# Hybrid conformer / PEER step: gathered rows for one token tile in both expert products, VectorE splits weights while gates are built

## Chip, cores and metric

One Trainium2 chip (trn2), one core. The metric is the device time of one execution in microseconds (us); the number given for a kernel is the median of its runs.

## What is computed (the reference, cut)

One layer, 512 + 32 = 544 tokens, width 2048, all float32. RMSNorm, one input projection, a conv branch and a differential-attention branch, a gated merge, an output projection with residual. Then the PEER channel mixer:

```
q  = h2 @ w_pq                          # 8 heads, two halves of 64
s1, s2 = q1 . sub_k1, q2 . sub_k2       # 128 keys each
v1, i1 = top16(s1); v2, i2 = top16(s2)
sc, j  = top16(v1[a] + v2[b])           # of 256 candidates
idx    = i1 * 128 + i2                  # 16384 experts
a      = einsum('td,thkd->thk', h2, u_tab[idx])
wgt    = softmax(sc) * gelu(a)
out    = einsum('thk,thkd->td', wgt, v_tab[idx])
```

Each token picks 8 x 16 = 128 experts of 16384.

## The kernel before

The 544 tokens lie on the free axis. Weights stream from `w_all` in 368 units of 1 MB (128 x 2048 float32), through two slots: SyncE loads a slot (`load_w`, L316), ScalarE rounds it to float32r (`hi`, L546), GpSimd or VectorE subtracts to get the low half (`lo` L482, `split` L1196), and TensorE multiplies high x high, low x high and high x low (`product`, L1271 to L1284). In the slot of unit m, unit m + 2 is prepared once m is done. The stages, in order:

1. **z stage**, 72 units, nine for each of the eight heads. VectorE empties PSUM (`evac`, L784), does rotary, softmax pieces and the 31 taps of the conv; between units' matmuls TensorE runs hooks (statistics, scores, transposes, values) that wait for VectorE and ScalarE. Beside each weight load SyncE copies two 1 MB units of `peer_v` inside DRAM (`rows_of`, L331) into a table with one expert per row, `v_rows`.
2. **Merge and out**, 16 + 16 units; each out unit gives `x2` and, at once, `h2_hi`/`h2_lo` without the norm's factor `rs2`, which is applied later: on `qp` (L1029) and, by GpSimd, on every result of the U stage (L500).
3. **peer_wq**, 8 units, then the **U stage**: 128 units, each the dot products of 128 experts with all 544 tokens, as two 272-column matmuls per weight tile (`u_unit`, L1485). ScalarE copies the result out of PSUM (L708), GpSimd scales it, ScalarE applies Gelu and stores it to `a_scr`. During the first 40 units VectorE does top-k for five token tiles, one per 8 units (L1064 to L1128); TensorE takes each tile's choices (`choices_t`, L1506) inside the seventh unit of the tile. Then 13 rounds of 6 units: VectorE makes one-hot rows for 32 tokens per round (L1147 to L1149) and TensorE multiplies them into gate tables (L1532); VectorE adds the two halves of the result into `g_st` (L1162, L1164).
4. **V stage**, 128 units in 16 groups of 8, for 416 tokens by 416-column matmuls (`v_group`, L1545), where VectorE prepares gate x activation (`prep`), adds each tile (L1192) and splits the weights. The first tile of 128 tokens (tokens 416 to 543) is done otherwise: GpSimd fetches each token's chosen rows of `v_rows` by indirect DMA (L506) and the chosen activations one by one from `a_scr` (L513), VectorE multiplies these by the gates (`weigh`, L1202) and accumulates the rows in PSUM (`gather_add`, L1208), nine rows a group.

Engines run in program order, so whatever stands behind a waiting instruction waits too.

## Time and profile before

| what | value |
|---|---|
| median of 3 runs | 4459.39 us (4457.0 to 4462.22) |
| the profiled execution | 4454.38 us, span 4452.6 us |
| mean granted TensorE clock | 0.989 |
| PE / DVE / ACT / POOL busy | 98% / 67% / 24% / 39% |
| DMA over the span | 822.58 MB, mean 185 GB/s |

The span runs from the first to the last instruction; 1.8 us lie outside it. Busy shares are means over stages with different limits, so the stretches and the timelines are read beside them.

### The profile page before, as it was taken

To read this page: it belongs to the slowest core of one execution; us is meant where nothing else is said; L and a number is where in the kernel's file an instruction comes from. 1 tells how busy PE (TensorE), PEld (TensorE's weight loads), DVE (VectorE), ACT (ScalarE), POOL (GpSimd) and SP (SyncE) were. 2 spreads that over 40 slices of the span, in tenths; PEclk is the share of its full clock that TensorE was granted. 3 is DMA by queue.
4 is the path that set the end of the run, shared out by engine and by line. 5 is a ranking of instruction groups with operands and counts; after the bars stand their busy time and mean duration, and the time that the engine had idled before them with its cause. 6 is when DMAs were issued, how large, how long until landed. Compare 5 with 4: busy or idle time off the path is not lost.

```text
span 4452.6 us, 78681 instructions
## 1 busy us (share of the span) xinstructions
PE 4351.6 (98%) x30758; PEld 4276.9 (96%) x30758; DVE 3003.3 (67%) x4653; ACT 1079.1 (24%) x1100; POOL 1758.2 (39%) x639
## 2 busy tenths in 40 slices
PE   8999999999999999999999999999989999999999
PEld 7999999999999999999999999999989999999999
DVE  5767656676762256557888888886268777877774
ACT  3332323322211122222222222222212121221221
POOL 3323323332333344444444444444544433444420
PEclk9999999999999999999999999999999999999999
DMA  6656566564333322222333333333577767776763
GB/s 241 235 191 229 197 234 229 188 227 164 106 136 135 110 95 108 108 106 102 133 126 136 131 130 135 134 135 128 198 277 264 291 261 292 266 296 258 282 253 126
DMA packets 332184, 822.58 MB, mean 185 GB/s; under 512 B 23152, under 2 KB 230768, under 8 KB 264688
## 3 DMA queue, kind: packets, MB, share of 16 engines
q1 hardware_dynamic: 279968, 608.53, 39.0%
q0 software_dynamic: 22528, 134.30, 7.4%
q10 hardware_dynamic: 29520, 77.40, 4.5%
q8 instruction: 119, 1.95, 0.2%
q14 instruction: 49, 0.40, 0.0%
HBM read 734.72 MB, written 219.66 MB: 214 GB/s over the span
## 4 chain that ended last, share of the span: by engine, by line
issue 56%; PE 21%; POOL 18%; DMA 3%; DVE 1%; POOLq 0%; ACT 0%; DVEq 0%; SPq 0%; ACTq 0%
PE pair L1557 21%; POOL w_lo L482 13%; POOL ab L500 4%; DMA a_el<-a_scr,a_idx 3%; POOL vg L506 1%; DVE ST L1208 1%; DVE acc L1192 0%; POOL a_el L513 0%; DMA xs<-x_t 0%; POOL xsq L488 0%; POOLq L481 0%; ACT h_hi L552 0%; POOLq L497 0%; POOLq L492 0%; DVE w_lo L1196 0%
## 5 line engine op out<-in xcount | busy, mean ns | idle before, releaser
L482 POOL TENSOR_TENSOR w_lo<-w_raw,w_hi 128x2048 fp32r<-128x2048 f32 x242 | 1118.0, 4620 | 1114.6 <-ACT w_hi L546 1114.6
L1280 PE MATMUL pair<-h_hi,w_hi 128*128 128x272 f32 x6656 | 1397.5, 291 | 12.8 <-issue 12.8
L1280 PE MATMUL pair<-h_hi,w_lo 128*128 128x272 f32 x6656 | 1381.5, 289 | 0.0
L1280 PE MATMUL pair<-h_lo,w_hi 128*128 128x272 f32 x6656 | 1377.0, 288 | 0.0
L1280 PEld LDWEIGHTS pair<-h_hi,w_hi 128*128 128x128 f32 x6656 | 1048.2, 189 | 21.1 <-issue 13.9
L1280 PEld LDWEIGHTS pair<-h_lo,w_hi 128*128 128x128 f32 x6656 | 1048.5, 189 | 0.0
L546 ACT ACTIVATE w_hi<-w_raw 128x2048 fp32r<-128x2048 f32 x368 | 703.8, 1913 | 1417.3 <-PE pair L1557 858.4
L1280 PEld LDWEIGHTS pair<-h_hi,w_lo 128*128 128x128 f32 x6656 | 1044.7, 189 | 0.0
L1557 PE MATMUL pair<-wt_hi,w_hi 128*128 128x416 f32 x2048 | 727.3, 355 | 49.4 <-DVE acc L1192 48.3
L1557 PE MATMUL pair<-wt_hi,w_lo 128*128 128x416 f32 x2048 | 728.7, 356 | 0.0
L1557 PE MATMUL pair<-wt_lo,w_hi 128*128 128x416 f32 x2048 | 722.6, 353 | 0.0
L506 POOL DMA_INDIRECT vg<-v_rows,v_idx x128 | 321.1, 2508 | 595.7 <-DVE ST L1208 584.9
L500 POOL TENSOR_TENSOR ab<-ab,rs 128x544 f32<-128x544 f32 x128 | 178.7, 1396 | 791.0 <-ACT ab L708 791.0
L1557 PEld LDWEIGHTS pair<-wt_hi,w_hi 128*128 128x128 f32 x2048 | 389.7, 190 | 57.3 <-DVE acc L1192 53.2
L1557 PEld LDWEIGHTS pair<-wt_lo,w_hi 128*128 128x128 f32 x2048 | 390.3, 191 | 6.3
L1557 PEld LDWEIGHTS pair<-wt_hi,w_lo 128*128 128x128 f32 x2048 | 389.5, 190 | 3.2
L708 ACT ACTIVATE ab<-pair 128x544 f32<-128x544 f32 x128 | 80.1, 626 | 1203.5 <-PE pair L1280 1203.5
L1148 DVE TENSOR_SCALAR oh<-late_sb,i_t,g_hi 128x128 fp32r<-128x128 f32 x416 | 356.5, 857 | 0.0
L877 DVE SCALAR_TENSOR_TENSOR xg<-u,params_sb,xg 128x512 f32<-128x512 f32 x464 | 338.6, 771 | 23.3 <-DVE xg L875 1.3
L1192 DVE TENSOR_TENSOR acc<-pair,acc 128x416 f32<-128x416 f32 x256 | 149.4, 588 | 277.0 <-PE pair L1557 218.0
L1208 DVE SCALAR_TENSOR_TENSOR ST<-vg,w_g,ST 128x2048 f32<-128x2048 f32 x128 | 300.6, 2348 | 2.9 <-DVE w_g L1202 2.9
L1196 DVE TENSOR_TENSOR w_lo<-w_raw,w_hi 128x2048 fp32r<-128x2048 f32 x126 | 287.9, 2285 | 13.3 <-ACT w_hi L546 13.3
(223 smaller groups left out, 3999.6 us busy)
## 6 DMA issues: line engine op xcount, KB each, us to landing
w_raw<-w_all SPq DMA_DIRECT2D x368, 1024.0 KB
v_rows<-w_all SPq DMA_DIRECT2D x128, 1024.0 KB, 8.8
a_scr<-gb ACTq DMA_DIRECT2D x128, 272.0 KB, 2.1
g_scr<-g_st ACTq DMA_DIRECT2D x26, 1024.0 KB, 4.1
a_st<-a_scr SPq DMA_DIRECT2D x16, 1664.0 KB, 8.4
gl_st<-g_scr SPq DMA_DIRECT2D x16, 1664.0 KB
gate_scr<-zb ACTq DMA_DIRECT2D x32, 272.0 KB, 2.2
gt<-gate_scr SPq DMA_DIRECT2D x32, 272.0 KB, 3.4
```

Source lines behind the costliest of these rows:

```text
L482: pool.tensor_tensor(w_lo[:, slot, :], raw[:, slot, :], w_hi[:, slot, :].bitcast(F32), ALU.subtract)\
L500: pool.tensor_tensor(ab[:, n, :], ab[:, n, :], rs2[:, :], ALU.mult).then_inc(ab_scaled, 1)
L506: pool.indirect_dma_start(vg[j % NVG][:, :], None, v_rows.rearrange("g c p d -> (g c p) d"), bass.IndirectOffsetOnAxis(v_idx[:, j:j + 1], ...
L546: act.activation(w_hi[:, slot, :], raw[:, slot, :], ACT.Copy).then_inc(hi_ready, 1)
L708: act.activation(two(ab[:, n, :]), PV[n], ACT.Copy).then_inc(ab_full, 1)
L877: own.by(V.scalar_tensor_tensor(xg[:, a:b], src, cw, xg[:, a:b], ALU.mult, ALU.add))
L1148: V.tensor_scalar(oh1[:, sl, 0, :], iota, c1, g_hi[:, bass.ds(t, 1)].bitcast(F32), ALU.is_equal, ALU.mult)
L1192: V.tensor_tensor(acc[:, d, 0:NT], PD[k], acc[:, d, 0:NT], ALU.add).then_inc(acc_added, 1)
L1196: V.tensor_tensor(w_lo[:, slot, :], raw[:, slot, :], w_hi[:, slot, :].bitcast(F32), ALU.subtract)\
L1208: V.scalar_tensor_tensor(acc_g, vg[x % NVG][:, :], w_g[:, bass.ds(s0 + x, 1)], acc_g, ALU.mult, ALU.add)\
L1280: last = mm(out[:, f, :], a, b[:, k, f * HT:(f + 1) * HT], start=(x == 0 and y == 0), stop=(x == n - 1 and y == 2))
L1557: last = mm(PD[k], a, r_[b][:, c, :], start=(c == 0 and y == 0), stop=(c == GRP - 1 and y == 2))
```

## The change

- **U stage for 416 tokens only.** `u_unit` now issues one 416-column matmul where there were two of 272. ScalarE applies Gelu straight from PSUM; the copy, GpSimd's scaling and `ab` are gone.
- **The other 128 tokens from fetched rows.** Each of their 128 dot products a token is made by VectorE (`dot`) from a row that GpSimd fetches, against `h2_g`, the tokens' `h2` turned to rows in PSUM by TensorE (`h2_turned`, 16 x 4 x 2 plain float32 matmuls with 32 columns). Nine dots stand in each of the 13 gate rounds, eleven behind them. The single-element fetches and `weigh` are gone; one Gelu and one multiply make `w_g`.
- **A row table for `peer_u`.** In the z stage SyncE loads each of the 128 units of `peer_u` into SBUF (`u_load`), VectorE transposes it in 32 x 32 blocks (`turn`, two ahead of each of the first sixteen `evac` of every eighteen), and SyncE stores it (`u_store`, four DMAs). For the room, the conv output and `o_lo` go to DRAM in the z stage and are loaded at the start of the merge, where the conv mean's matmuls now stand in the first unit's second tile.
- **The `v_rows` copies move** out of the z stage: 32 into the merge, 32 into the out units, two per unit over the eight peer_wq units and the first eight U units, one per unit over the 32 U units after.
- **h2 with its norm.** VectorE writes `h2_s`; when `rs2` is there it scales each of the 16 tiles, ScalarE rounds it, VectorE makes the low half, and the first two peer_wq units run side by side over k, waiting for each tile.
- **Low halves.** GpSimd makes them until the gate rounds (units up to 42 of U) and for the last 7 of U and first 2 of V; VectorE makes the 78 in the rounds (`split`) and, as before, those of the V stage.
- **Gates.** One plain float32 matmul of 128 columns a token where there was a float32r one of 256; ScalarE (`gate_copy`) empties PSUM instead of VectorE's copy and add. The rounds begin after 42 units.

```diff
-NVG = 3
+NG = 3
+DOTS = 9
...
+        UA = [PA[:, 2 * n, 0:NT] for n in range(2)]
+        PD = [ST[:, k, 0:NT] for k in range(2)]
         SV, TOV = S[:, :, 0:HT], TO[:, :, 0:HT]
...
+            def u_store(hp, i):
+                for q in range(4):
+                    sp.dma_start(u_rows[bass.ds(hp * 32 + i, 1), :, :, q, :].rearrange("a b i n -> i (a b) n"),
+                                 u_out[32 * q:32 * q + 32, i % 2, :].rearrange("p (b n) -> p b n", b=4)).then_inc(u_stored[i % 2], 16)
...
+                        for k in range(2):
+                            if n <= 16:
+                                sp.wait_ge(u_turned, hp * 32 + (2 * n + k + 1))
+                            if n < 16:
+                                u_load(hp, 2 * n + k)
+                            if 1 <= n <= 16:
+                                u_store(hp, 2 * n + k - 2)
...
+            g_end = (NQ + U_G0 + BU * NGB) // 2 + 2
+            pq_pu_loads(0, GRP, lambda v, n: [rows_at(v, NGRP // 4, GRP // 2 + 2 * n + k) for k in range(2)])
+            for g in range(NGRP // 4):
+                b0 = GRP + 4 * g
+                pq_pu_loads(b0, b0 + 4, lambda v, n: rows_late(v - b0, 3 * NGRP // 4 + g, n))
...
+                if j >= NG:
+                    pool.wait_ge(row_taken, j - NG + 1)
+                table = u_rows.rearrange("c b i q n -> (c b i) (q n)") if j < SLOTS else v_rows.rearrange("g c p d -> (g c p) d")
+                pool.indirect_dma_start(rows[j % NG][:, :], None, table,
+                                        bass.IndirectOffsetOnAxis(v_idx[:, j % SLOTS:j % SLOTS + 1], 0))\
+                    .then_inc(row_loaded[j % NG], 16)
...
+            for s in u_stored:
+                pool.wait_ge(s, 64 * NKEY // 2 + 1)
+            pool.wait_ge(scores_taken, TT)
+            pool.wait_ge(chosen, TT)
+            j = 0
+            for v in range(NGB // 2):
+                for k in range(3):
+                    for i in range(DOTS // 3):
+                        fetch(j)
+                        j += 1
+            w = U_PU + U_G0 + BU * NGB + 1
+            while w < U_PV + 2:
+                pool.wait_ge(lo_ready, w)
...
+                    if j < SLOTS:
...
-                act.activation(two(ab[:, n, :]), PV[n], ACT.Copy).then_inc(ab_full, 1)
+                act.wait_ge(a_stored[n], v * 16 + 1)
+                act.activation(gb[:, n, :], src[n], ACT.Gelu).then_inc(ab_full, 1)
                 hi(v + (U_PU // 2 + 1), n)
...
+                V.transpose(u_out[:, i % 2, :].rearrange("p (b k j) -> p k b j", b=4, k=KD), u_in[:, i % 2, :])\
+                    .then_inc(u_turned, 1)
...
+                for k in range(2):
+                    if ZPH * r + i < 16:
+                        turn(hp, 2 * (ZPH * r + i) + k)
...
+            for k in range(KD + 1):
+                if k < KD:
+                    V.tensor_tensor(h2_s[:, k, :], h2_s[:, k, :], rs2[:, :], ALU.mult).then_inc(h2_scaled, 1)
+                if k > 0:
+                    dve.wait_ge(h2_rounded, k)
+                    V.tensor_tensor(h2_lo[:, k - 1, :], h2_s[:, k - 1, :], h2_hi[:, k - 1, :].bitcast(F32), ALU.subtract)\
+                        .then_inc(h2_ready, 1)
...
-                    V.tensor_scalar(oh1[:, sl, 0, :], iota, c1, g_hi[:, bass.ds(t, 1)].bitcast(F32), ALU.is_equal, ALU.mult)
-                    ins = V.tensor_scalar(oh1[:, sl, 1, :], iota, c1, e_t[:, bass.ds(t, 1)], ALU.is_equal, ALU.mult)
+                    ins = V.tensor_scalar(oh1[:, sl, :], iota, c1, e_t[:, bass.ds(t, 1)], ALU.is_equal, ALU.mult)
...
+            def split(un, slot):
+                dve.wait_ge(hi_ready, un + 1)
+                dve.wait_ge(lo_ready, un)
+                V.tensor_tensor(w_lo[:, slot, :], raw[:, slot, :], w_hi[:, slot, :].bitcast(F32), ALU.subtract)\
+                    .then_inc(lo_ready, 1)
...
+                j = v * DOTS + i
+                dve.wait_ge(row_loaded[i % NG], v * (16 * DOTS // NG) + 16 * (i // NG + 1))
+                buf = rows[i % NG]
+                V.scalar_tensor_tensor(buf[:, :], buf[:, :], 1.0, h2_g, ALU.mult, ALU.mult,
+                                       accum_out=dot_g[:, bass.ds(j, 1)]).then_inc(row_taken, 1)
...
+                un = v * 6 + (U_PU + U_G0 + 1)
+                dots = iter(range(DOTS))
+                for b in range(2):
+                    for i in range(BU):
+                        split(un + (BU * b + i), (BU * b + i + 1) % 2)
+                        dot(v, next(dots))
+                        next_hot(4 * b + i)
+                        if i < 2 - b:
+                            dot(v, next(dots))
+                    next_hot(4 * b + 3)
...
+            dve.wait_ge(h2g_ready, 1)
...
+            for i in range(SLOTS - NGB // 2 * DOTS):
+                dot(NGB // 2, i)
...
+            dve.wait_ge(a_g_ready, 1)
+            own.by(V.tensor_tensor(w_g[:, :], gate_g[:, :], a_el[:, :], ALU.mult))
...
+            pe.wait_ge(osum_ready, 1)
+            spread(S, ones, osq).then_inc(ostat_ready, 1)
...
+            for k in range(KD):
+                pe.wait_ge(h2_ready, k + 1)
+                for n in range(2):
+                    wh, wl = (w[:, n, k * P:(k + 1) * P] for w in (w_hi, w_lo))
...
+                    if k == KD - 1:
+                        last.then_inc(unit_done, 1)
...
+                for k in range(KD):
+                    wh, wl = (w[:, n, k * P:(k + 1) * P] for w in (w_hi, w_lo))
+                    for y, (a, b) in enumerate(((wh, h2_hi), (wh, h2_lo), (wl, h2_hi))):
+                        last = mm(dst[n], a, b[:, k, 0:NT], start=(k == 0 and y == 0), stop=(k == KD - 1 and y == 2))
...
+                for k in range(KD):
+                    for q in range(4):
+                        for y, src in enumerate((h2_hi, h2_lo)):
+                            last = mm(PA[:, q, 32 * k:32 * k + 32], src[:, k, NT:T].bitcast(F32), ident[:, 32 * q:32 * q + 32],
+                                      start=(y == 0), stop=(y == 1))
+                last.then_inc(h2g_ready, 1)
...
+                            out = ST[:, 2 + gq % 2, :].rearrange("p (c t) -> p c t", t=4)[:, :, t]
+                            last = mm(out, oh2[:, sl, :], oh1[:, sl, :], start=True, stop=True)
```

## Rows read from the trace of the kernel before

**Rows 1.** Stretches (us, busy us of each engine, clock, DMA share, GB/s).

```profile
35.00:1100.00 1065.00, 1047.72 (x7816) 998.93 (x7816) 701.19 (x996) 318.54 (x474) 330.68 (x72) 0.99 0.61 210
...
1604.00:3217.00 1613.00, 1611.56 (x12878) 1609.51 (x12878) 1161.93 (x2526) 404.14 (x413) 768.71 (x256) 1.00 0.35 127
3217.00:4452.00 1235.00, 1183.95 (x6160) 1166.46 (x6160) 892.40 (x887) 243.64 (x128) 456.02 (x258) 0.98 0.70 261
```

**Rows 2.** Timeline of ScalarE, two unit ends in the tail of the U stage.

```profile
3179.95 0.63 ACT L708 ACTIVATE ab<-pair 128x544 f32<-128x544 f32 x1 [9.05 <-PE pair L1280]
...
3191.97 0.63 ACT L708 ACTIVATE ab<-pair 128x544 f32<-128x544 f32 x1 [9.05 <-PE pair L1280]
```

**Rows 3.** Timeline of ScalarE, unit ends while the gate matmuls run.

```profile
2511.79 0.63 ACT L708 ACTIVATE ab<-pair 128x544 f32<-128x544 f32 x1 [9.69 <-PE pair L1280]
...
2549.87 0.62 ACT L708 ACTIVATE ab<-pair 128x544 f32<-128x544 f32 x1 [9.69 <-PE pair L1280]
```

**Rows 4.** Timeline of PE, V stage, 55 matmul starts apart.

```profile
3863.76 0.35 PE L1557 MATMUL pair<-wt_lo,w_hi 128*128 128x416 f32 x1
...
3874.17 0.35 PE L1557 MATMUL pair<-wt_hi,w_lo 128*128 128x416 f32 x1
```

**Rows 5.** The page's part 5, TensorE in the V stage and VectorE's long operations.

```profile
L1557 PE MATMUL pair<-wt_hi,w_hi 128*128 128x416 f32 x2048 | 727.3, 355 | 49.4 <-DVE acc L1192 48.3
...
L1208 DVE SCALAR_TENSOR_TENSOR ST<-vg,w_g,ST 128x2048 f32<-128x2048 f32 x128 | 300.6, 2348 | 2.9 <-DVE w_g L1202 2.9
L1196 DVE TENSOR_TENSOR w_lo<-w_raw,w_hi 128x2048 fp32r<-128x2048 f32 x126 | 287.9, 2285 | 13.3 <-ACT w_hi L546 13.3
```

**Rows 6.** Waits in the V stage, summed (us, times, longest).

```profile
DVE w_g L1202 <- DMA a_el<-a_scr,a_idx: 89.7, 14, 14.3
```

**Rows 7.** Timeline of PE, plain f32 matmuls of the attention (two instructions each).

```profile
1033.86 0.61 PE L1378 MATMUL ST<-a_t,v_tok 128*128 128x128 f32 x4
1034.39 0.91 PE L1347 MATMUL ST<-kn_t,q_t 64*128 64x384 f32 x2
...
685.40 0.53 PE L1381 MATMUL ST<-a_t,pv 128*128 128x32 f32 x4
685.86 0.40 PE L1382 MATMUL ST<-a_t,v_smp 32*128 32x32 f32 x2
```

**Rows 8.** Timeline of VectorE, one top-k tile, first copy to last reduction.

```profile
1707.89 1.22 DVE L1066 COPY sc<-ST 128x1024 f32<-128x1024 f32 x1 [20.32 <-PE ST L1499]
...
1759.15 6.22 DVE L1112 TENSOR_TENSOR wk<-jf,late_sb 128x2048 f32<-128x2048 f32 x1
...
1767.73 2.29 DVE L1120 TENSOR_REDUCE isel<-wk 128x128 f32<-128x2048 f32 x1
```

**Rows 9.** Timeline of GpSimd, the low half of one unit's weights.

```profile
1722.53 4.63 POOL L482 TENSOR_TENSOR w_lo<-w_raw,w_hi 128x2048 fp32r<-128x2048 f32 x1 [0.43 <-ACT w_hi L546]
```

**Rows 10.** Timeline of VectorE, end of a head; then ScalarE, its unit's end.

```profile
704.25 0.72 DVE L808 TENSOR_TENSOR zb<-pair,rs 128x544 f32<-128x544 f32 x1
...
696.52 1.92 ACT L546 ACTIVATE w_hi<-w_raw 128x2048 fp32r<-128x2048 f32 x1 [2.38 <-PE pair L1280]
```

**Rows 11.** The page's parts 3 and 6, DMA queues and the row copies.

```profile
q1 hardware_dynamic: 279968, 608.53, 39.0%
...
v_rows<-w_all SPq DMA_DIRECT2D x128, 1024.0 KB, 8.8
```

**Rows 12.** Timeline of VectorE and GpSimd between the out units and peer_wq.

```profile
1503.68 0.72 DVE L1009 SCALAR_TENSOR_TENSOR x<-pair,xt 128x544 f32<-128x544 f32 x1 [8.23 <-PE pair L1280]
...
1514.08 3.55 DVE L1024 RECIPROCAL rs<-rs 128x544 f32<-128x544 f32 x1 [2.02 <-ACT rs L695]
...
1507.08 4.67 POOL L482 TENSOR_TENSOR w_lo<-w_raw,w_hi 128x2048 fp32r<-128x2048 f32 x1 [7.18 <-ACT w_hi L546]
```

**Rows 13.** Groups of VectorE by line, the one-hot rows (busy us, mean ns).

```profile
L1149 DVE TENSOR_SCALAR oh<-late_sb,i_t,e_t 128x128 fp32r<-128x128 f32 x416 | 184.4, 443 | 0.0
...
L1147 DVE TENSOR_SCALAR oh<-late_sb,i_t 128x128 fp32r<-128x128 f32 x416 | 155.8, 375 | 0.0
```

More of the change, by code:

```diff
@@ L158, in build @@
         rs1 = az.take("rs1", [P, T])
+        c_ts = az.take("c_ts", [P, TS])
         xs = Area(Y0, HALF).take("xs", [P, KD, T])
@@ L225, in build @@
         g_st = aw.take("g_st", [P, 2, NKEY, GB])
-        oh2 = aw.take("oh2", [P, 8, NKEY], F32R)
-        oh1 = aw.take("oh1", [P, 8, 2, NKEY], F32R)
+        oh2 = aw.take("oh2", [P, 16, NKEY])
+        oh1 = aw.take("oh1", [P, 16, NKEY])
         avx, avy = Area(X0, BIG), Area(Y0, BIG)
         acc = avx.take("acc", [P, KD, T])
+        rows = [avy.take(f"rows{i}", [P, DM]) for i in range(2)] + [rows2]
         a_st = avy.take("a_st", [P, GRP, NT])
@@ L397, in _ @@
                 merge_loads(v, KD, 0)
+                for n in range(GRP // 2):
+                    rows_at(v, 0, n)
             with sp.Fori(0, NC_ // 2) as v:
                 merge_loads(v, 0, KD)
+                for n in range(GRP // 2, GRP):
+                    rows_at(v, 0, n)
             sp.wait_ge(m_taken, 2 + 2 * KD)
@@ L404, in _ @@
                 for n in range(2):
+                    for k in range(GRP // 4):
+                        rows_at(v, NGRP // 4, n * (GRP // 4) + k)
                     sp.wait_ge(lo_ready, v * 2 + (n + 1 + U_OUT))
@@ L518, in _ @@
[L518 to L532 removed]
+            lo(U_PU + U_G0, 0)
@@ new lines, in _ @@
+            for s in u_stored:
+                pool.wait_ge(s, 64 * NKEY // 2 + 1)
[10 more added lines that the diff above has]
+                pool.wait_ge(lo_ready, w)
+                lo(w, w % 2)
+                w += 1
+                for i in range(2):
+                    if j < SLOTS:
+                        fetch(j)
+                        j += 1
@@ L535, in _ @@
+            pool.wait_ge(rows_stored, 16 * NV)
+            for j in range(SLOTS, 2 * SLOTS):
+                fetch(j)
         @block.scalar
@@ L1218, in group @@
             def group(g, parity, more, slots, splits, pre=None):
-                s0, full, rounds, n_slots = slots
+                s0, rounds, n_slots = slots
                 for n in range(GRP):
@@ L1233, in group @@
                             prep(1 - parity, 2 * (n - 3) + 1)
-                    if n == 0 and n_slots:
-                        weigh(parity, s0 + parity * PER_GRP, full, n_slots)
-                        settle()
                     if n < n_slots:
@@ L1411, in _, with mean @@
                         product(PV[n % 2], n % 2, 0, range(KD), h_hi, h_lo, order(hooks, i)).then_inc(unit_done, 1)
-            pe.wait_ge(std_ready, 3 * NH + 2)
-            pe.wait_ge(conv_done, NH + 1)
-            for k in range(KC):
-                last = spread(S, ones, c_all[:, k, :], start=(k == 0), stop=(k == KC - 1))
-            last.then_inc(mean_ready, 1)
             pe.wait_ge(zb_full, NZ + 2)
             pe.wait_ge(norm_done, 3 * NH + 1)
+            pe.wait_ge(o_loaded[0], 16)
+            def mean():
+                pe.wait_ge(std_ready, 3 * NH + 2)
+                pe.wait_ge(c_loaded, 16)
+                for k in range(KC):
+                    last = spread(S, ones, c_all[:, k, :], start=(k == 0), stop=(k == KC - 1))
+                last.then_inc(mean_ready, 1)
             def merge_unit(v, n, unit0, rhs_hi, rhs_lo, hooks=None):
@@ L1426, in merge_unit @@
                     product(PV[k], n, KC * k, range(KC), rhs_hi, rhs_lo, hooks and hooks[k]).then_inc(tile_done, 1)
-            with pe.Fori(0, NA // 4) as v:
+            for n in range(2):
+                merge_unit(0, n, 0, o_hi, o_lo, ({KC - 2: lambda: pe.wait_ge(o_loaded[1], 16)}, {KC - 1: mean}) if n == 0 else None)
+            with pe.Fori(1, NA // 4) as v:
                 for n in range(2):
@@ L1474, in _ @@
                 pe.wait_ge(x2_ready, n + 1 + NO)
-                hooks = {7: rms2, KD - 2: lambda: pe.wait_ge(h2_ready, KD)} if n == 0 else None
-                product(PV[n], n, 0, range(KD), h2_hi, h2_lo, hooks).then_inc(unit_done, 1)
+            for k in range(KD):
+                pe.wait_ge(h2_ready, k + 1)
+                for n in range(2):
+                    wh, wl = (w[:, n, k * P:(k + 1) * P] for w in (w_hi, w_lo))
+                    for y, (a, b) in enumerate(((wh, h2_hi), (wh, h2_lo), (wl, h2_hi))):
+                        for f in range(2):
+                            last = mm(PV[n][:, f, :], a, b[:, k, f * HT:(f + 1) * HT],
+                                      start=(k == 0 and y == 0), stop=(k == KD - 1 and y == 2))
+                    if k == KD - 1:
+                        last.then_inc(unit_done, 1)
             with pe.Fori(1, NQ // 2) as v:
@@ L1565, in _ @@
             for d in range(KD):
-                last = nc.tensor.transpose(ST[:, d // 4, (d % 4) * GT:(d % 4 + 1) * GT], vg[0][:, d * P:(d + 1) * P], ident)
+                last = nc.tensor.transpose(PA[:, d // 4, (d % 4) * GT:(d % 4 + 1) * GT], rows[0][:, d * P:(d + 1) * P], ident)
             last.then_inc(acc_g_turned, 1)
```

282 lines of the change are left out of this document (139 added, 143 removed).

## Prediction, made before the changed kernel was run

> **What bounds the kernel now.** I read first the busy time by stretch, then TensorE's pace inside each stage, then who waits for whom. In the U stage TensorE is busy 1611.56 of 1613 us at a clock of 1.00 [rows 1]: nothing but its own instructions sets the time there. In the V stage it is busy 1183.95 of 1235 us [rows 1], and the missing 50 us are waits for VectorE's adds, 48.3 us [rows 5], which stand behind `weigh`, waiting 14 times and 89.7 us for single fetched elements [rows 6]. The z stage is nearly full too (1047.72 of 1065 us), but VectorE is at 701.19 us and the DMA engines at 0.61 there [rows 1]. So a gain has to come out of TensorE's columns in U, and whatever is loaded onto VectorE and the DMAs in z has to fit there.
>
> **The paces.** A U unit takes 3191.97 - 3179.95 = 12.02 us [rows 2] for 96 matmuls of 272 columns, 0.125 us each. A 416-column matmul takes 10.41 / 55 = 0.1893 us [rows 4]; 48 of them make a unit of 9.09 us. While gates run, a unit takes (2549.87 - 2511.79) / 3 = 12.69 us [rows 3], 0.67 us more, so all 78 units pay 52 us for gates.
>
> **U stage, term by term.**
> - The products: 128 x (12.02 - 9.09) = **-375**.
> - Gates: 416 matmuls of plain float32, two instructions each. Four instructions of 128 columns took 1034.39 - 1033.86 = 0.53 us [rows 7], so 0.265 a token, 110 us for 52: **+58**. The lower bound is the four 32-column instructions, 0.46 us [rows 7], which would give 96 us (+44).
> - `h2_turned`: 16 x 4 x 2 matmuls of two instructions, 256 x 0.115 = 29 us [rows 7], bare, because the round's first split and dot wait for it: **+29** (34 at the 128-column pace).
> - Top-k: from first copy to last reduction a tile takes 1767.73 + 2.29 - 1707.89 = 62.1 us on VectorE [rows 8]. TensorE takes the choices a quarter into the seventh unit, now after 6.25 x 9.09 = 56.8 us instead of 75. Part of the 62.1 is blocking: the second L1112 took 6.22 us [rows 8] where the like-sized L1196 takes 2.285 [rows 5], and it ends when a GpSimd low half ends. GpSimd still does one such 4.63 us operation a unit [rows 9], so I keep 61. Four tiles stall by 4: **+17** (0 to 30). The first tile has no such hook.
> - Low halves: with GpSimd the slot of a unit is ready 0.5 + 1.9 + 4.6 = 7.0 us (Gelu, a little less than the 0.63 of 544 columns [rows 2]; rounding [rows 10]; low half [rows 9]) after the unit before ends, against 9.09. Hidden, with 2 us to spare; VectorE's two-input operations can hold GpSimd off by 2.3, so some tenths a tile. In the last eight units GpSimd has a low half and two fetches to do, near 9 us: **+2**.
> - DMA at the start: two copies, a weight load and a store are 3.36 MB a unit of 9.5 us (scores included), 354 GB/s, where q1 moved 608.53 MB in 39.0% of 4452.6 us, 350 GB/s [rows 11]: **+5** (0 to 10).
> Sum for U: **-264**.
>
> **The gate rounds on VectorE.** A round of TensorE is 6 x 9.09 + 32 x 0.265 = 63.0 us. VectorE has six splits of 2.285, nine dots of about 2.35 [rows 5] and 32 pairs of one-hots, at most 0.375 + 0.443 = 0.82 us a pair [rows 13], blocked ones included: 13.7 + 21.1 + 26.2 = 61 us, and about 50 when GpSimd no longer blocks. Each split is due 5 us before TensorE needs it. So I cost this at nothing; the cover is 2 to 13 us a round. Rows cannot run dry: nine a round is one per 7 us with three buffers, and V already fetches one per 9 us. ScalarE's `gate_copy`, Gelu and rounding are near 3 us of a 10.5 us unit.
>
> **V stage.** `weigh` goes: the 48.3 us of stalls, and with them the clock that falls behind them (0.98 over the stage against 1.00 in U [rows 1], so short times at the lower of its two levels, 1.2 instead of 2.4 GHz): TensorE was busy 1183.95 us where 6144 x 0.1893 is 1163, 21 us too long. What is late next is the first row of V, fetched only after GpSimd's last low half (7 us into V) and needed before VectorE's split for the third unit: about 5 us. **-62** (-50 to -69).
>
> **Out to peer_wq.** h2 can't be used before `rs2`. The last x2 begins at 1503.68 and the reciprocal ends at 1514.08 + 3.55 [rows 12], of which about 4.4 us are a copy blocked by the GpSimd operation of 1507.08 [rows 12]; with one VectorE operation fewer ahead of it that copy just slips past. Scale, round and subtract add 2.2. TensorE idles about 11.5 us, and 16 if the copy is caught. Then both first units end together and GpSimd must finish the next slot, 6.7 us more. Clock recovery about 4. **+22** (16 to 32).
>
> **z to merge.** The last head's conv output and `o_lo` go out and come back (2.5 MB behind one another) before the seventh k tile of the first product: **+8** (0 to 15). The mean's matmuls only move. The `v_rows` copies in merge and out I cost at nothing: two a unit of 12 us or more is what z carried beside its loads at a share of 0.61 [rows 1].
>
> **z stage, the uncertain term.** No row shows a `turn`. From below it is 2.285 us, the f32 operation over as many elements [rows 5]; from above twice that, 4.6. I take 2.3: one input, no conversion. The Trainium skill has the only price of it: Vector Engine (DVE) Microarchitecture Reference, section 3.8, says that the transposing front end is "Pipelined to sustain one element per cycle per lane"; an estimate by it is the time of any other operation over 2048 elements at that rate, and the sum would stay. VectorE has 701.19 / 8 = 87.6 us a head of 133 [rows 1]; sixteen turns make it 124. They stand before `evac`, partly in time that VectorE waits. But at a head's end VectorE is late already: `evac` of the ninth unit began at 704.25, while the unit had ended by 696.52 [rows 10]; there the turns push it to some 13 us late, past a unit's 12.02, and in between softmax weights miss their hooks by 0.5 to 2 us each. Following one head through I get some 6 us of TensorE waits: 48. DMA: z moved 1065 x 210 = 224 MB; less 134 of copies, plus 268 in and out and 4, is 362 MB. At 210 / 0.61 = 344 GB/s [rows 1] that is 1052 us busy, 92% of the longer stage, and a turn waits for its load and for its buffer's store: 16. The clock falls at some of the new stalls: 16. **+80** (+15 to +200).
>
> **Sum.** -264 - 62 + 22 + 8 + 80 = -216. The profiled execution took 4454.38 us (span 4452.6); the median of the runs is 4459.39, 5.0 more. 4454.4 - 216 = 4238, as a median **4243 us**.
>
> **Rivals.**
> - *z absorbs the turns* (12%): VectorE's waits in z, 365 us by the busy time [rows 1], swallow 295 us of turns; +15 instead of +80: 4178. Against it: the late `evac` [rows 10].
> - *z becomes bound by VectorE and the DMA chain together* (12%): load, turn and store have two buffers each and both resources are above 90%; +190: 4353.
> - *The rounds become bound by VectorE* (7%): a round of 70 us instead of 63, because dots wait for rows or splits come behind one-hots: 13 x 7 = 91: 4334.
> - *The end on the other side: the turn is dear* (7%). Without z the change is at -296, 37 us a head. VectorE's head is 87.6 + 16 turns + some 8 us of waits that nothing can fill; it reaches 133 + 37 at a turn of 4.6 us. From there the kernel is slower; at 5.5 us z grows by 8 x (183.6 - 133) = 405: 4568. Only a transpose at less than half the rate of any like operation here [rows 5] does that.
> - *Memory bandwidth* (4%). A copy inside DRAM reads and writes: a unit of peer_wq and the first eight of U would move 5.45 MB at the memory. If that ran at the 336 GB/s that z shows in this count ((224 + 134) / 1065) it would be 16 us a unit instead of 12 and 9.5, 85 us in all: 4328. The copies landed 8.8 us after issue [rows 11], and a load and two copies go out within some 1.5 us: over 500 GB/s, so I give it little. The Trainium skill speaks for it: SBUF — State Buffer, "A bandwidth-pool intuition that's wrong", puts HBM to one core at ~358 GB/s; by that the estimate is 15.2 us a unit and +71. The 8.8 us row disagrees.
>
> **Chances.** Forecast 58%, its own range 4195 to 4300. The range to hold 8 of 10 takes in the first three rivals: **4165 to 4375**. About 0.2%, 9 us, is what can be told from no change. Faster 0.92, same 0.01, slower 0.07, the dear turn being the only case that ends there.
>
> **What would show it.** Right: U units 9.09 us apart; rounds of 63 us; turns of 2.3 us; V groups 72.7 us apart with no wait for acc; TensorE idle some 12 and 7 us around the first peer_wq units; z longer by 40 to 120 us with waits of TensorE for VectorE's values in the later units of a head. Wrong: turns above 3 us; DMA share of z at 0.97 or more; rounds above 66 us with VectorE busy; weight loads late (ScalarE waiting for w_raw) in z or at the start of U.

## The result, and the profile after

The changed kernel took **4356.7 us** (median of 4 runs, 4353.33 to 4363.76), the kernel before 4458.19 beside it (median of 4 runs): a ratio of 0.9775 (0.9758 to 0.9792), 101.5 us faster. The prediction was 4243 us, 216 faster, with a range of 4165 to 4375: the direction was right and the time lies in the range, but the gain is 101.5 us where 216 were forecast.

Where it went is read from the times at which TensorE begins each stage (merge: its first product; U: the first scores; V: its first product):

| stage | before | after | difference | forecast |
|---|---|---|---|---|
| z, to merge's first product | 1100.5 | 1249.6 | +149 | +80, and part of the +8 |
| merge, out, peer_wq | 503.9 | 540.0 | +36 | +22, and the rest of the +8 |
| U | 1612.7 | 1380.2 | -232 | -264 |
| V, to the end | 1235.5 | 1181.3 | -54 | -62 |

TensorE began merge behind a wait of 2.30 us before and of 9.26 us after:

```profile
1100.51 0.64 PE L1280 MATMUL pair<-o_hi,w_hi 128*128 128x272 f32 x2 [2.30 <-DVE zb L808]
```

```profile
1249.63 0.82 PE L1376 MATMUL PA<-o_hi,w_hi 128*128 128x272 f32 x2 [9.26 <-DVE zb L903]
```

The stretches of the profile after, which answer to [rows 1] (start and end in us, length, busy time and instruction count of each engine, granted clock, DMA share, GB/s):

```profile
35.00:1241.00 1206.00, 1073.74 (x7784) 1014.33 (x7784) 927.85 (x1120) 314.20 (x473) 325.94 (x71) 0.95 0.87 304
1249.00:1789.00 540.00, 506.23 (x3880) 501.85 (x3880) 224.15 (x247) 105.59 (x80) 180.76 (x39) 0.96 0.81 280
1789.00:3169.00 1380.00, 1341.72 (x7406) 1323.29 (x7406) 989.99 (x2229) 377.63 (x388) 370.53 (x182) 0.97 0.75 271
3169.00:4351.00 1182.00, 1167.10 (x6160) 1155.28 (x6160) 890.25 (x874) 241.76 (x126) 304.32 (x125) 0.99 0.73 276
```

The z stage was nearly full before, 17 us idle in 1065. Now TensorE idles 132 of 1206 us there, and its work takes 26 us longer at a clock of 0.95. U was full before; now 38 us of it are idle. Who makes it wait, over the whole span (who waits <- for whom: total us, times, longest):

```profile
PE ST L1390 <- ACT sq L646: 52.9, 12, 12.7
PE ST L1461 <- DVE e L946: 46.7, 17, 5.4
PE PA L1376 <- DVE zb L903: 16.9, 5, 9.3
PE ST L1631 <- DVE isel L1215: 14.4, 4, 3.6
PE ST L1682 <- DVE wt_lo L1291: 12.6, 1, 12.6
PE PA L1376 <- issue: 11.9, 3, 4.4
PE ST L1390 <- ACT xsq L615: 11.9, 1, 11.9
PE ST L1598 <- POOL w_lo L542: 11.6, 1, 11.6
PE ST L1682 <- DVE acc L1295: 11.0, 1, 11.0
```

The first two are z. ScalarE's square is late because VectorE's evac is; in each of the four passes (two heads each) TensorE stood 11 to 13 us at the second head's first statistics. Of the third, 9.3 us are the seam of z and merge. The fourth is top-k. The sixth stands between the passes of z, the seventh at the kernel's start, and the rest at seams between stages. The costliest groups of VectorE on the page that are new:

```profile
L872 DVE STREAM_TRANSPOSE u_out<-u_in 128x2048 f32<-128x2048 f32 x128 | 291.1, 2296 | 105.9 <-DMA u_rows<-u_out 92.3
L1253 DVE SCALAR_TENSOR_TENSOR rows<-rows,PA 128x2048 f32<-128x2048 f32 x128 | 291.9, 2281 | 53.8 <-DMA rows<-u_rows,v_idx 53.8
```

A turn takes 2.296 us, as assumed, so the dear turn (the case on the slow side) is out. The Trainium skill (Vector Engine (DVE) Microarchitecture Reference, section 3.8) has a transpose at one element per cycle and lane, and the trace agrees: `dot`, over as many elements, takes 2.281. But the turns also *waited* 92.3 us for stores of the table, which is VectorE's time as well.

`h2_turned` is the next surprise. The view of instructions of 2200 to 2290 us, and the stretch of 2220 to 2240:

```profile
L1608 PE MATMUL PA<-consts_sb,h_lo 128*128 128x32 f32 x128 | 36.9, 380 | 0.0
L1608 PE MATMUL PA<-consts_sb,h_hi 128*128 128x32 f32 x128 | 36.7, 379 | 0.0
```

```profile
2220.00:2240.00 20.00, 20.00 (x96) 20.00 (x95) 0.00 (x0) 0.00 (x0) 0.00 (x0) 0.50 0.12 50
```

The 256 instructions ran from 2211.7 to 2261.7 us, 50 us and not 29: 96 of them in 20 us at a granted clock of 0.50, the lower level of 1.2 GHz, with TensorE never idle. In the 10 us before the block the clock was 1.00.

The gate rounds went as forecast: ScalarE's Gelus of seven units in a row lie (2760.4 - 2698.4) / 6 = 10.33 us apart, 62.0 us a round against 63.0.

```profile
L779 ACT ACTIVATE gb<-ST x7: 517/517/521, 2698.4 to 2760.4; 128x416 f32<-128x416 f32 x7
```

At the seam of U and V the timeline of TensorE shows three stalls that end within 57 us (start, length, instruction, idle time before it and what ended it):

```profile
3136.42 0.71 PE L1598 MATMUL ST<-h_hi,w_hi 128*128 128x416 f32 x1 [11.56 <-POOL w_lo L542]
...
3169.80 0.71 PE L1682 MATMUL ST<-wt_hi,w_hi 128*128 128x416 f32 x1 [12.59 <-DVE wt_lo L1291]
...
3192.85 0.72 PE L1682 MATMUL ST<-wt_hi,w_hi 128*128 128x416 f32 x1 [11.00 <-DVE acc L1295]
```

All three go back to loads that came late. The weight unit behind the loads for V's first group landed late, so its low half was late. GpSimd's next row fetch stands behind that low half, VectorE's dot waited for the row, and the first preparation stands behind the dots. VectorE's first add of V waited for `acc`, which SyncE loads behind the second group's loads:

```profile
3129.73 1.91 ACT L606 ACTIVATE w_hi<-w_raw 128x2048 fp32r<-128x2048 f32 x1 [13.29 <-DMA w_raw<-w_all]
```

```profile
3143.70 2.29 DVE L1253 SCALAR_TENSOR_TENSOR rows<-rows,PA 128x2048 f32<-128x2048 f32 x1 [15.86 <-DMA rows<-u_rows,v_idx]
...
3192.20 1.09 DVE L1295 TENSOR_TENSOR acc<-ST,acc 128x416 f32<-128x416 f32 x2 [22.44 <-DMA acc<-x_scr]
```

### The profile page after: what moved, and what is told of

It is laid out like the page before. It is cut to its first block, busy times and chain, and to the rows that moved or that the text cites. A ratio compares the mean times of both kernels' runs of the same rounds, so it can differ in the third digit from the quotient of the medians.

```text
span 4351.1 us, 69418 instructions
## 1 busy us (share of the span) xinstructions
PE 4106.5 (94%) x25286; PEld 4007.7 (92%) x25286; DVE 3063.5 (70%) x4486; ACT 1059.2 (24%) x1090; POOL 1207.5 (28%) x433
## 4 chain that ended last, share of the span: by engine, by line
PE 53%; issue 33%; POOL 6%; DVE 6%; DMA 1%; SPq 0%; ACT 0%; POOLq 0%; DVEq 0%; ACTq 0%
PE ST L1682 27%; PE ST L1598 18%; POOL w_lo L542 6%; PE PA L1598 3%; PE ST L1657 2%; PE PA L1376 2%; PE PA L1608 1%; DVE wk L1207 1%; DMA w_raw<-w_all 1%; DVE cand L1177 1%; DVE wk L1211 0%; DVE isel L1215 0%; DVE ti L1173 0%; DVE ti L1176 0%; DVE wk L1169 0%
## 5 line engine op out<-in xcount | busy, mean ns | idle before, releaser
L1682 PE MATMUL ST<-wt_hi,w_hi 128*128 128x416 f32 x2048 | 719.5, 351 | 23.6 <-DVE wt_lo L1291 12.6
L1682 PE MATMUL ST<-wt_hi,w_lo 128*128 128x416 f32 x2048 | 724.5, 354 | 0.0
L1682 PE MATMUL ST<-wt_lo,w_hi 128*128 128x416 f32 x2048 | 716.5, 350 | 0.0
L1376 PE MATMUL PA<-h_hi,w_hi 128*128 128x272 f32 x2496 | 546.4, 301 | 25.6 <-issue 11.9
L1598 PE MATMUL ST<-h_hi,w_hi 128*128 128x416 f32 x1408 | 533.4, 379 | 11.6 <-POOL w_lo L542 11.6
L1376 PE MATMUL PA<-h_hi,w_lo 128*128 128x272 f32 x2496 | 524.4, 292 | 0.0
L1376 PE MATMUL PA<-h_lo,w_hi 128*128 128x272 f32 x2496 | 524.3, 292 | 0.0
L1598 PE MATMUL ST<-h_lo,w_hi 128*128 128x416 f32 x1408 | 499.4, 355 | 0.0
L1598 PE MATMUL ST<-h_hi,w_lo 128*128 128x416 f32 x1408 | 496.7, 353 | 0.0
L1376 PEld LDWEIGHTS PA<-h_hi,w_hi 128*128 128x128 f32 x2496 | 404.7, 194 | 34.9 <-issue 27.1
L872 DVE STREAM_TRANSPOSE u_out<-u_in 128x2048 f32<-128x2048 f32 x128 | 291.1, 2296 | 105.9 <-DMA u_rows<-u_out 92.3
```

The costliest lines, as they stand in the source:

```text
L872: V.transpose(u_out[:, i % 2, :].rearrange("p (b k j) -> p k b j", b=4, k=KD), u_in[:, i % 2, :])\
L1376: last = mm(out[:, f, :], a, b[:, k, f * HT:(f + 1) * HT], start=(x == 0 and y == 0), stop=(x == n - 1 and y == 2))
L1598: last = mm(dst[n], a, b[:, k, 0:NT], start=(k == 0 and y == 0), stop=(k == KD - 1 and y == 2))
L1682: last = mm(PD[k], a, r_[b][:, c, :], start=(c == 0 and y == 0), stop=(c == GRP - 1 and y == 2))
```

## Experiments: what the table costs in the z stage

Theory V says that VectorE's time and order make z longer, theory D that the DMAs do. The first three runs take the new work of the z stage apart: without both turns and moves (loads and stores), with the turns alone, and with the moves alone.

**No table.**

```diff
-                        for k in range(2):
-                            if n <= 16:
-                                sp.wait_ge(u_turned, ...)
...
-                for k in range(2):
-                    if ZPH * r + i < 16:
-                        turn(hp, 2 * (ZPH * r + i) + k)
-                table = u_rows... if j < SLOTS else v_rows...
+                table = v_rows...
```

> The z stage of the changed kernel without the table of peer_u: no loads, no turns, no stores. The dot products of the first tile fetch from v_rows in place of u_rows, so they are left wrong, at the same cost. In the changed kernel the first product of the merge starts at 1249.6 us of the span, in the kernel before at 1100.5. Both theories (VectorE's order, DMA traffic) say that the whole difference of 149 us is the table's: merge from 1100 to 1110 us, and the time 4210 to 4225 us. If the conv output and o_lo that go out to DRAM cost in the z stage, the merge starts later than 1120.

**Turns only.** As above, but the turns stay and read two units that are loaded once.

> The z stage with all 128 turns on VectorE, but no loads and stores of the table (two units are loaded once, and each turn reads them again; the dot products fetch from v_rows and are wrong). Theory V, VectorE's time and order: the turns stand ahead of evac, 128 x 2.3 us on VectorE, and the heads' last units are late by them; merge starts at 1200 to 1240 us, the time is 4305 to 4345. Theory D, the DMAs: turns waited 92.3 us for stores of u_rows and the queues are at a share of 0.87; merge starts at 1110 to 1150 us, the time is 4215 to 4255.

**Moves only.**

```diff
-                V.transpose(u_out[:, i % 2, :].rearrange("p (b k j) -> p k b j", b=4, k=KD), u_in[:, i % 2, :])
+                V.transpose(u_out[:, i % 2, 0:32], u_in[:, i % 2, 0:32])
```

> The z stage with all loads and stores of the table, but each turn cut to 32 of its 2048 columns, so that VectorE has all waits and almost none of the work (the table is left wrong). Theory V: merge starts at 1105 to 1140 us, time 4210 to 4245. Theory D: merge starts at 1190 to 1240 us, time 4295 to 4345. A result in the middle of both this run and the one without moves says that both are needed, each adding to the other.

They took 4187.45, 4253.91 and 4295.32 us (2 runs each). The first product of merge, in the same order:

```profile
1085.43 0.82 PE L1362 MATMUL PA<-o_hi,w_hi 128*128 128x272 f32 x2 [9.25 <-DVE zb L889]
```

```profile
1148.51 0.82 PE L1370 MATMUL PA<-o_hi,w_hi 128*128 128x272 f32 x2 [9.26 <-DVE zb L895]
```

```profile
1175.63 0.82 PE L1379 MATMUL PA<-o_hi,w_hi 128*128 128x272 f32 x2 [8.33 <-DVE zb L903]
```

The table costs 1249.6 - 1085.4 = 164 us of z. That is 15 more than the difference to the kernel before, for without the table z is 15 us shorter than before (1085.4 against 1100.5). The turns alone cost 63 and the moves alone 90, together 153 of the 164: neither theory has it alone, and my expectations for the two single runs were both too one-sided. The run without table came out below its range too (4187 against 4210 to 4225). The changed kernel's own merge began between 1249.6 and 1261.0 us in five profiles, so the 11 us between 153 and 164 say nothing. The moves cost far more than the 16 us that I gave to the DMAs. How they do it stands in VectorE's group for the turns of the third run, 35 to 1100 us:

```profile
L872 DVE STREAM_TRANSPOSE u_out<-u_in 128x32 f32<-128x32 f32 x122 | 23.4, 203 | 191.2 <-DMA u_rows<-u_out 179.3 <-issue 10.7 <-DMA u_in<-w_all 0.8
```

The turns, of 0.2 us each, still wait 179.3 us in all for the store of two turns ago, and they stand *ahead of evac*. So a late transfer is passed on to VectorE, evac and TensorE.

**Other places for the turns.** None at the ninth unit of a head, two in each of the first eight, and in the first two units behind evac.

```diff
-                for k in range(2):
-                    if ZPH * r + i < 16:
-                        turn(hp, 2 * (ZPH * r + i) + k)
+                if 2 <= i < 8:
+                    turns()
...
                     V.tensor_tensor(two(zb[:, j, :]), PV[j], two(rs1[:, :]), ALU.mult).then_inc(zb_full, 1)
+                if i < 2:
+                    turns()
```

> The changed kernel with other places for the turns, nothing else: none at the ninth unit of either head, two in each of the first eight; those of a head's first two units stand behind evac, in VectorE's wait for ScalarE's rstd, in place of ahead of it. The stall of 11 to 13 us in each of the four passes, at the second head's first statistics, stands behind evac of the ninth unit and four turns. Theory V: it goes, and some of the others shrink, 35 to 60 us less, 4295 to 4320. Theory D: the same bytes in the same time, within 10 us of 4357.

4285.79 us, ratio to before 0.9610 (0.9594 to 0.9626): 71 us less than the changed kernel, with the same work and the same bytes. Merge began at 1181.3, and the 11 to 13 us stalls were gone. TensorE's waits and VectorE's, 35 to 1165 us:

```profile
PE ST L1466 <- DVE e L951: 43.8, 15, 5.6
PE ST L1428 <- DVE zb L906: 11.1, 8, 2.3
```

```profile
DVE u_out L872 <- DMA u_rows<-u_out: 77.2, 42, 3.9
```

**Moves only, in these places.** Both edits together.

> The turns moved in pairs, each cut to 32 columns: all loads and stores, VectorE free of the work (the table is left wrong). With full turns in these places merge started at 1181.3 us; with cut turns in the old places at 1175.6; without the table at 1085.4. If the bytes (DMA share 0.9) bound the z stage: merge at 1165 to 1180 here too, 4268 to 4284. If the waits for loads and stores only count with VectorE's own work and place: merge at 1100 to 1130, 4205 to 4235.

4250.16 us (2 runs), and merge began at 1124.0:

```profile
1124.02 0.82 PE L1384 MATMUL PA<-o_hi,w_hi 128*128 128x272 f32 x2 [9.25 <-DVE zb L906]
```

All the bytes of the table fit in a z stage only 39 us longer than without them, at a DMA share of 0.93 (35 to 1115 us), so the bytes alone don't make the 1181.3 of the run with full turns. The whole account of z, in us over the run without table:

| places of the turns | turns only | moves only | both |
|---|---|---|---|
| as changed | 63 | 90 | 164 |
| moved | not run | 39 | 96 |

The places cost 68 of the 164 us, shown by one edit. Which part of it does this (none at the ninth unit, or the first two behind evac) no run splits. What is left, 96, is about the moves' 39 and the turns' 63, but that 63 was measured in the old places.

**Turns one by one.** The 16 turns of a head spread through the head, and each store issued ahead of the next load; then the same with the old order of load and store.

```diff
+                    evac(hp, r, 0)
+                    TN(0)
+                    rope(h, 0)
+                    TN(1)
...
+                        att_max(g + s, s)
+                        TN(2 * s + 4)
+                        att_mix(g + s, s)
+                        TN(2 * s + 5)
```

> The changed kernel with its 16 turns a head spread one by one through the head: behind evac and rope, in VectorE's wait for the exponentials between the maximum and the mix of the first two tiles, and behind each mix of the last three; SyncE issues each store ahead of the next load. With the turns moved in pairs merge started at 1181.3 us, 96 later than without the table, and with cut turns at 1175.6. If what is left there is the bytes (DMA share 0.91 to 0.92), this run gains nothing on that one: 4280 to 4290 us. If it is turns that stand in pairs and wait for a store just issued (73.8 us of waits there), merge starts at 1140 to 1165 and the time is 4250 to 4275.

> The run with the turns spread one by one, but with SyncE's old order, each load ahead of the store. That run was 13 us slower than the changed kernel, its turns waiting 173 us for loads, where stores went first. If the order of load and store did that: at or below the run with turns moved in pairs, 4270 to 4290. If the single places did it: 4350 or more.

The first missed both of its cases: 4369.75 us (ratio 0.9803, 0.9788 to 0.9818). The second, 4346.63 (0.9764, 0.9745 to 0.9782), came 3 us under the one for single places, 4350 or more. With stores first VectorE waited for loads instead; with loads first, again for stores (35 to 1240 and to 1165 us):

```profile
DVE u_out L872 <- DMA u_in<-w_all: 173.0, 47, 15.0
```

```profile
DVE u_out L872 <- DMA u_rows<-u_out: 92.6, 39, 4.1
```

The order of load and store is worth 23 us, by these two runs. With the same order, the single places lose 61 us against the pairs moved. Some of that is at the stage's end, where TensorE stood 30.0 us ahead of merge in place of 9.3. That the last head's turns, now behind its last evac, hold back the loads of `o_lo` and the conv output is my reading; no run isolates it.

## Experiments: h2_turned and the seam

**h2_turned in 16 pieces**, one behind each k step of the unit (`{k: (lambda k=k: h2_turned(k)) for k in range(KD)}` in place of `{KD - 1: h2_turned}`).

> The changed kernel with h2_turned cut into 16 pieces of 16 matmuls, one behind each k step of the unit that it stood behind. The same 256 matmuls took 50 us there in one block at a granted clock of 0.56, and 0.115 us each is 29 us. Theory C, the clock: among matmuls of 416 columns it stays at 1.00 and the unit takes 9.1 + 29 us: 20 to 25 us less than the changed kernel, 4332 to 4337. Theory I, the pitch of 0.195 us is each matmul's own, with its weight load: no change within 8 us of 4357.

4370.41 us (0.9808, 0.9792 to 0.9823), neither theory's number, and the U stage 5 us *longer* (1385.5). The clock fell here too, and the wide matmuls between the narrow ones slowed with it. A stretch in the middle of the unit:

```profile
2240.00:2250.00 10.00, 10.00 (x44) 9.87 (x43) 0.00 (x0) 0.00 (x0) 0.00 (x0) 0.50 0.00 0
```

**h2_turned by 128 columns.**

```diff
                 for k in range(KD):
-                    for q in range(4):
-                        for y, src in enumerate((h2_hi, h2_lo)):
-                            last = mm(PA[:, q, 32 * k:32 * k + 32], src[...], ident[:, 32 * q:32 * q + 32], ...)
+                    for y, src in enumerate((h2_hi, h2_lo)):
+                        last = mm(PA[:, k // 4, P * (k % 4):P * (k % 4 + 1)], src[...], ident, ...)
...
+            for q in range(4):
+                own.by(V.tensor_copy(stage[:, q], turned[:, q]))
+            settle()
+            V.tensor_copy(h2_g, rows2[:, :]).then_inc(h2g_placed, 1)
```

> The changed kernel with h2_turned as 32 plain float32 products of 128 columns in place of 128 of 32; VectorE then puts the result in the order of the rows with four copies through the third row buffer and one back, about 5 us, beside TensorE's next unit. Cut in pieces, the 256 narrow matmuls brought the granted clock down to 0.50 inside a unit of 416-column matmuls, so the narrow ones themselves are the suspect. Theory N, the number of narrow instructions sets the cost: 64 instructions of 128 columns at 0.13 us are 8.5 us where 50 were, 35 to 42 us less, 4315 to 4322 us. Theory F, plain float32 of any width brings the clock down: the block takes 17 us and the next unit is slow too, 20 to 28 us less.

4333.19 us (0.9731, 0.9716 to 0.9746), 23.5 less. The stage itself gained more: U took 1332.7 us against 1380.2, 47.5 less, but z and what follows it took 12 us more in this run than in the changed kernel's profile with the same code, and V 12 more. The same values moved by 64 instructions, in stretch 2220 to 2230, with the clock at 1.00:

```profile
2220.00:2230.00 10.00, 10.00 (x81) 9.98 (x80) 0.47 (x1) 2.31 (x2) 2.37 (x3) 1.00 0.85 322
```

By the whole time alone this would be theory F's number (20 to 28 us); the stage and the clock decide for N, whose 35 to 42 us were short by 5. The block is short, though, 7 us. The gate rounds of the changed kernel have 32 such products a round, each alone among nine wide matmuls, and the clock stays at 1.00 there; a long unbroken block of 128-column plain float32 is in no run:

```profile
2290.00:3079.00 789.00, 789.00 (x4480) 780.25 (x4479) 603.29 (x1085) 233.98 (x253) 111.71 (x113) 1.00 0.82 303
```

**The seam of U and V.**

```diff
-            load_ag(0)
-            pq_pu_loads(g_end, (NQ + NU) // 2)
+            for v in range(g_end, (NQ + NU) // 2):
+                for n in range(2):
+                    sp.wait_ge(lo_ready, v * 2 + (n + 1 + U_PQ))
+                    load_w(v + (U_PQ // 2 + 1), n)
+                    if v == g_end:
+                        (load_a, load_gl)[n](0)
...
             for c in range(GRP):
                 prep(0, c)
+                if c % 2:
+                    dot(NGB // 2, tail - 4 + c // 2)
```

> The changed kernel with another order at the seam of U and V: the first group's a and gates are loaded one behind each of two weight units, not both ahead of them; VectorE prepares the first group between the last four dot products and clears acc_g behind that; behind the seam the first weight units and x2 go ahead of the second group's a and gates. In the changed kernel TensorE waited 11.56 us for a low half at 3136, 12.59 for the first preparation and 11.00 for acc. If the order of the queue and of VectorE makes them: 20 to 30 us less, 4327 to 4337. If it is the bytes at that place, whatever the order: within 10 us of 4357.

4344.6 us (0.9743, 0.9727 to 0.9760): 12 less, half of what I expected. The stall for acc was gone and the one for the first preparation was 9.34 us, but one of 11.73 us for a low half stood in U as before. A new wait had taken the old one's place: the first preparation waited for `gl_st`, the four dots stood behind it, and GpSimd's next fetch, which stands ahead of a low half in its program, waited for a row buffer:

```profile
3146.19 0.59 DVE L1301 TENSOR_TENSOR a_st<-a_st,gl_st 128x416 f32<-128x416 f32 x1 [17.79 <-DMA gl_st<-g_scr]
```

```profile
3151.84 1.06 POOL L580 DMA_INDIRECT rows<-u_rows,v_idx  x1 [16.95 <-DVE rows L1267]
```

**All three.** Turns one by one with stores first, h2_turned in pieces, and this seam.

> The three edits together (turns spread, h2_turned in pieces, seam of U and V reordered). They lie in three stages, so their gains should add: 4357 less what each gives alone, about 4357 - 90 - 22 - 25 = 4220 us, within 10 us of the sum of the single gains.

4363.21 us (0.9790, 0.9777 to 0.9804). Single differences of +13, +14 and -12 add to 4372; the edits add within 9 us, but two of them were losses.

**The best version.** Turns moved in pairs, h2_turned by 128 columns, the seam with all dots ahead of the first preparation and `gl_st` loaded first, and `{9: choices_t}` for `{3: choices_t}` (with `{5: gate_sums}` for `{1: gate_sums}`).

> Turns moved in pairs, h2_turned by 128 columns, the seam of U and V reordered with all dots ahead of the first preparation, and the token tiles' choices taken at the tenth instead of the fourth k step. Gains over the changed kernel in its own stages: 71 us, some 38, some 20 and 4 x 3.6 = 14: 4357 - 143 = 4214 us, 4200 to 4230 if they add.

**4214.38 us** (5 runs, 4209.54 to 4219.78), 0.9458 (0.9445 to 0.9471): as expected, 142 us below the changed kernel, with nothing of the computation left out. The sum fits better than its terms: between the two profiles z lost 70 us, U 77 and V nothing (1184.6 against 1181.3), where 71, 52 and some 20 for the seam had been added up. U takes 1303.4 us, 29 less than with the 128-column turn alone; merge starts at 1179.9. Of the U stage's 11.6 us for a low half 3.7 are left, of 14.4 for choices 0.8, and the first waits for acc come to 12.6 us in eight pieces, the longest 2.6.

**The changed kernel again, and two more turns moved.** In the last run two turns of each head stand in VectorE's waits for the first two tiles' exponentials.

> The changed kernel, unaltered, on the same chip as the run beside it: the time of merge's start there is the spread of the z stage between chips. 4353 to 4368 us; merge starts at 1247 to 1262 us.

> The run with all four edits, and in z two turns of each head moved out of the pairs ahead of the fourth and fifth evac into VectorE's waits for the first two tiles' exponentials (3.7 and 2.3 us there). In that run TensorE waited 45.5 us, 16 times, for attention weights, above all 5.2 to 5.7 us for the third tile's in each head. If VectorE's order makes that wait: it shrinks to some 1 to 3 us, 16 to 35 us less, 4180 to 4200 us, merge at 1145 to 1165. If bytes bound the stage by now: the wait moves elsewhere, within 8 us of 4214.

4360.76 us (0.9781, 0.9764 to 0.9797), with merge at 1256.5, and 4209.86 (4199.93 to 4217.69; 0.9447, 0.9428 to 0.9465), which the spread can't tell from the best version. The turns' waits for stores went from 74.5 to 137.7 us, and TensorE's for attention weights only from 45.5 to 38.2 (35 to 1150 us of both):

```profile
DVE u_out L888 <- DMA u_rows<-u_out: 137.7, 54, 5.3
```

```profile
PE ST L1492 <- DVE e L969: 38.2, 16, 4.2
```

A turn that comes earlier only waits longer for its output buffer's store, so VectorE's order no longer makes the wait: the 4180 to 4200 us of that case didn't come, the "within 8 us of 4214" of the other did. I read it as the chain of store and turn through two buffers that holds z there. The share of the DMA engines is 0.91 in both runs, so the bytes remain a rival. A third output buffer would tell them apart; it wasn't tried.

## Why the prediction was right or wrong

- **z, +80: the step that failed.** The term was built of 48 us of late VectorE, 16 of DMA waits and 16 of clock. The turns alone cost 63 us, near 48 and some clock. But the moves alone cost 90, where I had 16. I had "a turn waits for its load and for its buffer's store" in the text, and priced it as a small extra on a busy resource. The runs showed in its place that each wait is inserted into VectorE's program ahead of evac and delays all that is behind; of the cost, 68 us are the places alone, and with the new places the 11 to 13 us stalls behind a head's end are gone, where [rows 10] had shown VectorE already late. The clock took more than 16: from the run without table to the changed kernel TensorE's busy time in z goes from 1033.87 to 1073.74 us for the same number of matmuls, 40 us, at 1.00 and 0.95. The run without table, to lay beside the first stretch above:

```profile
35.00:1076.00 1041.00, 1033.87 (x7786) 986.31 (x7784) 697.59 (x992) 315.14 (x472) 326.90 (x72) 1.00 0.27 94
```

- The rival "z bound by VectorE and the DMA chain together" gave 4353, and the time was 4356.7. That the numbers meet is luck: it had +190 for z where +149 came, and the other stages fell 46 us short of their sum. Its mechanism, two buffers and both resources loaded, is the nearest of all. Its claim that both are above 90% isn't: the DMA share is 0.87, and VectorE is busy for 77% of the stretch. The waits in VectorE's program did it, and no share shows a full resource.
- **U, -264: -232.** The difference of 32 is a net one: three terms below were 43 us too small (21 for `h2_turned`, 10 for the late low half, 12.6 ahead of V), others some 21 too large (the rounds 13 times 1 us, the DMAs 5, top-k 3); the 10 us left I can't place. The products came as forecast (Gelus of units without extra work 8.98 and 9.15 us apart, 9.07 in the mean, against 9.09), the rounds with 62.0 for 63.0, top-k with 3.6 us for 4 a tile. The +5 for the DMAs at the start doesn't show: no unit of the first eight waited for its weights. `h2_turned` was the wrong term: 0.115 us an instruction came from four matmuls at full clock [rows 7], and 256 of them are not that row; +21. The end of U had +2 for low halves; it cost 11.6, and not by GpSimd's work but by SyncE's queue: 3.3 MB for V's first group stood ahead of a weight load. The late rows and the 12.59 us ahead of V, for which no term stood, follow from the same load. In the kernel before the same loads stood there, under units of 12 us. I named no cover for them, and the change took it away.
- **V, -62: -54.** `weigh` and its waits are gone. But 11.35 us of the 48.3 that I called its stalls [rows 5] were the first wait for acc in the trace before, which has nothing to do with it, and 11.00 are still there:

```profile
3246.84 0.72 PE L1557 MATMUL pair<-wt_hi,w_hi 128*128 128x416 f32 x1 [11.35 <-DVE acc L1192]
```

  The stall before V's first product, 12.59 us, is in the table's U; the row fetched late, for which I had 5 us, doesn't show.
- **Out to peer_wq and z to merge, +22 and +8.** TensorE's idle times around `rs2` are 3.4, 6.7 and 6.0 us, as the steps had them. With 5.1 us for `o_lo` and the clock behind each of them (0.75 and 0.83 after out, 0.76 and 0.84 after z) the two seams cost 36 us and the 7 that z's end grew by: 43 against 30.
- **Memory bandwidth** as a bound is out: while two copies and a weight unit move in each peer_wq unit, TensorE is busy all of the time. From 1714.5 to 1788.5 us six units took 12.3 us each, not 16. With each copy read and written that is 5.24 MB a unit, by estimate some 425 GB/s at the memory.

```profile
1720.00:1740.00 20.00, 20.00 (x161) 20.00 (x161) 0.72 (x1) 1.92 (x1) 4.58 (x1) 1.00 0.87 300
```

## What to carry to other kernels

When work with a DMA on both sides is put into an engine's program, price the wait for its buffers as time of that engine, and ask what stands behind it at each place; the same work and bytes cost 68 us more in one set of places than in another. A term taken from a handful of instructions at full clock doesn't hold for hundreds of them in a row: look for what fewer, wider ones would do. And where a stage gets shorter, list the transfers that its old length covered.

## What the runs showed of the hardware that was not expected

- The granted clock falls to 0.50 under plain float32 matmuls of 32 columns that follow each other without idle time, and 416-column matmuls between them slow down as well (in the run in pieces they start 0.35 us apart instead of 0.19). With the same values moved by 128-column matmuls it stayed at 1.00. Whether the width or the number of instructions does it isn't shown: both were changed at once.
- A stage with the same code differs between runs by 11 us. Merge began at 1249.6, 1256.5, 1259.8, 1261.0 and 1255.4 us in five profiles with the changed kernel's z stage. V took 1181.3 us in the changed kernel's profile, 1192.9 in the run with the 128-column turn and 1200.8 in the one with moved cut turns, all with the same code of V. A difference of 10 or 20 us between two runs is therefore not read as an effect where the edited stage doesn't show it.
- VectorE's two-input operations are held off whole by one of GpSimd. The prediction had counted on it from [rows 8], with one slip: the 6.22 us operation there doesn't end with the low half (1758.61 to 1763.23 us), it ends 2.14 us behind it, about its own time (2.29 us at its quickest). In the run with the new seam GpSimd made two low halves, 9.38 us for both; a subtraction over 416 columns that takes 0.59 us took 5.36 beside the first, and the multiplication behind it 4.95 beside the second. The Trainium skill has this rule (SBUF — State Buffer, "SBUF: two separate sides": whichever starts first has the port pair for its whole instruction, and the other is blocked). The trace agrees that one waits for the whole of the other; who came first it doesn't settle, for the subtraction is recorded 0.40 us ahead of the low half.

```profile
3152.52 5.36 DVE L1306 TENSOR_TENSOR wt_lo<-a_st,wt_hi 128x416 fp32r<-128x416 f32 x1
...
3157.80 4.95 DVE L1301 TENSOR_TENSOR a_st<-a_st,gl_st 128x416 f32<-128x416 f32 x1
```
